# The order of loads and of square sums in the head of a four-layer trunk: x in front of the modulation tiles, its sums among the middle ones

## What is computed

```
for i in range(DEPTH):                     # mixers: conv, pool, attn, conv
    mod_p = adaln(c_ctx[None, :], ada_w[i], ada_b[i])     # silu(c) @ w + b, six blocks of 1024
    mod_s = adaln(c, ada_w[i], ada_b[i])
    hp = modulate(rms_norm(xp, norm1_w[i]), mod_p[0], mod_p[1])   # x * (1 + scale) + shift
    hs = modulate(rms_norm(xs, norm1_w[i]), mod_s[0], mod_s[1])
    ...                                    # mixer on hp and hs
    xp = xp + mod_p[2] * mp
    xs = xs + mod_s[2] * ms
    ...                                    # the same with mod 3 to 5 around a SwiGLU FFN
```

## Time and profile before

| | us |
|---|---|
| median of 3 runs | 2781.82 |
| lowest and highest | 2777.01 and 2784.19 |
| the profiled execution | 2776.66 |
| its span on the core | 2774.3 |
| mean granted TensorE clock, of 1 | 0.988 |

### The profile page before, as it was taken

One profiled execution on the slowest core, in us unless ns is written; L12 is line 12 of the kernel. 1 busy time (PEld: TensorE's weight loads), 2 busy tenths in 40 slices (PEclk: granted clock), 3 DMA queues, 4 the chain that ended last, 5 costly groups with the idle time before them and its releaser, 6 DMA issues.

```text
span 2774.3 us, 46075 instructions
## 1 busy us (share of the span) xinstructions
PE 2675.9 (96%) x17562; PEld 2605.7 (94%) x17562; DVE 1756.7 (63%) x3033; ACT 859.0 (31%) x1174; POOL 103.2 (4%) x199
## 2 busy tenths in 40 slices
PE   7998999999969999999988999999999999999997
PEld 7998999999959999999954999999999999999996
DVE  6888868775587776746665477767465554334344
ACT  3222332322343223124345332231242233223122
POOL 1000000000000000000000000000000000000000
PEclk9999999999989999999999999999999999999998
DMA  7344335343113443412100334434122222222111
GB/s 282 129 140 147 128 126 179 129 159 108 46 52 129 141 158 133 152 66 80 50 1 0 114 129 144 159 128 152 66 78 76 76 69 76 76 76 76 69 68 61
DMA packets 84442, 293.31 MB, mean 106 GB/s; under 512 B 9984, under 2 KB 12416, under 8 KB 84224
## 3 DMA queue, kind: packets, MB, share of 16 engines
q1 hardware_dynamic: 58000, 196.09, 20.7%
q0 software_dynamic: 26352, 95.96, 10.0%
HBM read 289.13 MB, written 2.88 MB: 105 GB/s over the span
## 4 chain that ended last, share of the span: by engine, by line
PE 89%; DVE 6%; ACT 2%; issue 2%; DMA 1%; DVEq 0%; ACTq 0%; POOL 0%; POOLq 0%
PE ps L395 50%; PE ps L394 34%; PE ps_x L502 1%; PE ps L481 1%; DVE w_lo L843 1%; DVE tmp L914 1%; ACT w_hi L595 1%; DVE g_lo L857 1%; DVE tmp L922 1%; DMA ada_w<-in_ada_w 1%; PE ps_sum L492 0%; DVE ps_x L871 0%; ACT tmp L736 0%; PE ps_x L469 0%; ACT g_hi L607 0%
## 5 line engine op out<-in xcount | busy, mean ns | idle before, releaser
L843 DVE TENSOR_TENSOR w_lo<-raw,w_hi 128x1024 fp32r<-128x1024 f32 (+2 forms) x364 | 430.9, 1184 | 687.0 <-ACT w_hi L595 682.9
L595 ACT ACTIVATE w_hi<-raw 128x1024 fp32r<-128x1024 f32 (+2 forms) x364 | 373.5, 1026 | 937.8 <-PE ps L395 937.4
L395 PE MATMUL ps<-h_hi,w_hi 128*128 128x386 f32 x1904 | 649.6, 341 | 0.0
L395 PE MATMUL ps<-h_lo,w_hi 128*128 128x386 f32 x1904 | 645.8, 339 | 0.0
L395 PE MATMUL ps<-h_hi,w_lo 128*128 128x386 f32 x1904 | 644.1, 338 | 0.0
L394 PE MATMUL ps<-h_hi,w_hi 128*128 128x256 f32 x1904 | 546.7, 287 | 22.1 <-DVE h_lo L978 14.9
L394 PE MATMUL ps<-h_lo,w_hi 128*128 128x256 f32 x1904 | 536.4, 282 | 0.0
L394 PE MATMUL ps<-h_hi,w_lo 128*128 128x256 f32 x1904 | 536.2, 282 | 0.0
L871 DVE CUSTOM_DVE_ANT_0 ps_x<-ada_w,cond 128x1024 f32<-128x1024 f32 x366 | 450.6, 1231 | 47.1 <-DVE tmp L914 16.4
L394 PEld LDWEIGHTS ps<-h_hi,w_hi 128*128 128x128 f32 x1904 | 361.4, 190 | 28.9 <-DVE h_lo L978 12.9
L395 PEld LDWEIGHTS ps<-h_hi,w_hi 128*128 128x128 f32 x1904 | 361.2, 190 | 3.0 <-issue 2.0
(11 more groups left out here) (123 smaller groups left out, 2736.4 us busy)
## 6 DMA issues: line engine op xcount, KB each, us to landing
raw<-in_weights SPq DMA_DIRECT2D x324, 512.0 KB, 3.2
ada_w<-in_ada_w POOLq DMA_DIRECT2D x183, 512.0 KB, 3.5
raw<-in_weights SPq DMA_DIRECT2D x32, 384.0 KB, 2.9
mix<-in_ada_head SPq DMA_DIRECT2D x9, 512.0 KB, 8.9
x<-in_x SPq DMA_DIRECT2D x4, 640.0 KB, 9.8
out_y<-mix SPq DMA_DIRECT2D x8, 320.0 KB, 2.3
cond<-in_cond SPq DMA_DIRECT2D x1, 1024.0 KB, 4.8
raw<-in_weights SPq DMA_DIRECT2D x8, 128.0 KB, 2.3
```

The costliest lines, as they stand in the source:

```text
L395: mm = pe.matmul(ps[:, 2 * slot + 1, 0:width - TA], w[:, slot, ws], a(k)[:, TA:width], start=begin, stop=end)
L595: act.activation(w_hi[:, j % 2, 0:tiles * P], raw[:, j, 0:tiles * P], ACT.Copy).then_inc(w_hi_ready, 1)
L843: dve.tensor_tensor(w_lo[:, j % 2, 0:tiles * P], raw[:, j, 0:tiles * P], w_hi[:, j % 2, 0:tiles * P].bitcast(F32), ALU.subtract).then_inc( ...
```

## The change

On SP, tables and all of x are issued right after head tile 0, and tiles 1 to 8 follow; units 2 and 3 (with rope, cache_v and all behind them) wait for PE's last tile. On GpSimd, triples 1 and 2 are written out as before, and triple 3 and later ones wait for PE's last tile. On PE, two sums each stand in front of tiles 3 to 6 instead of 5 to 8. Nothing is added to or taken from the computation.

```
+SUM_FROM = 3
...
-            for n in range(ADA_PE):
+            load_head(0)
+            load_consts()
+            for n in range(X_PIECES):
+                piece = slice(n * KD // X_PIECES, (n + 1) * KD // X_PIECES)
+                sp.dma_start(x[:, piece, :], d["x"][:, piece, :]).then_inc(x_in, 16)
+            for n in range(1, ADA_PE):
                 if n > 1:
 
                     sp.wait_ge(ada_step, 2 * n - 2)
                 load_head(n)
-                if n == 1:
-                    load_consts()
-                if 0 < n <= X_PIECES:
-                    piece = slice((n - 1) * KD // X_PIECES, n * KD // X_PIECES)
-                    sp.dma_start(x[:, piece, :], d["x"][:, piece, :]).then_inc(x_in, 16)
                 if n == ADA_PE - 3:
                     load_raw(0, (0, 1))
+
+            sp.wait_ge(head_tile, ADA_PE)
             load_raw(0, (2, 3))
...
-            with pool.Fori(1, attn_q) as i:
+            for i in range(1, ADA_HEAD):
+                for j in range(ADA_N):
+                    load_ada(i, j)
+
+            pool.wait_ge(head_tile, ADA_PE)
+            with pool.Fori(ADA_HEAD, attn_q) as i:
                 for j in range(ADA_N):
                     load_ada(i, j)
...
-                if n == ADA_PE - KD // 2:
+                if n == SUM_FROM:
                     pe.wait_ge(ones_ready, 2)
-                if n >= ADA_PE - KD // 2:
-
-                    for m in (2 * (n - ADA_PE) + KD, 2 * (n - ADA_PE) + KD + 1):
+                if SUM_FROM <= n < SUM_FROM + KD // 2:
+
+                    for m in (2 * (n - SUM_FROM), 2 * (n - SUM_FROM) + 1):
                         sum_squares(0, m)
```

## The result

| | before | changed |
|---|---|---|
| median, us | 2779.01 (12 runs) | 2783.15 (12 runs) |
| lowest and highest | 2776.41, 2784.19 | 2780.00, 2789.80 |
| ratio, 95% interval | | 1.0016, 1.0008 to 1.0023 |
| profiled execution | 2776.66 | 2783.87 |
| its span | 2774.3 | 2781.8 |

The changed kernel is 0.16% slower, 4.1 us by the medians. That is within the 0.3% that I called no change, and of the sign and about the size of the forecast (+3.2).

The account below looks back on a forecast made before the run. The prediction took PE, not loads, to bound the head's last 17.6 us. Its terms, 0 + 3 + 0 + 0.2 = +3.2 us on the first product's start, took the median from 2781.82 to 2785.0, range 2778 to 2793.

Parts of the forecast that it names:

- PE bounds the head from 31.5 us: Head before the first product: PE, not its loads, binds from 31.56 to 49.15 us, without a break.
- Rival B: Head: loads, not PE, set the end, so the change gains 8 us, to 2774; chance 5%.
- Tile 1 behind x: Head loads: x complete at 21.5 us, tile 1 lands at 23.8; PE idle 11.6 us instead of 5.2.
- The warm tiles 3 and 4 against the idle time: PE's head: 6.4 us more idle against 3.8 saved by two tiles at full clock; +2.8 us by the count of ends.
- The cold tail: Last three head tiles, no sums after: clock falls near 51.5 us, +0 to 0.4; upper end +3.8.
- rival D: Last three head tiles: clock falls right away, two tiles cost 1.89 us more each; +7 in all, 2789; chance 8%.
- The first unit: Behind the first product: no cost of its own forecast; everything there simply moves along with the first product.
- When the clock rises: First square sums in the head: clock may rise up to 3.4 us later, 0 to +1.7; 0 to +1 taken.
- Rival C: Head: clock does not rise in the first sums, every part behind them at half clock; +23 us, 2805; chance 4%.
- The loads put off: Loads issued after PE's last head tile: unit 2 and triple 3 hidden by 3.5 to 8 us, cost 0.
- The sum: Start of the first product: 0 + 3 + 0 + 0.2 = +3.2 us, all behind it moving along; median 2785.0.

Follow-up runs that it names:

- e3: Kernel before with only PE's order changed, two sums ahead of tiles 3 to 6; 2782.20 against 2777.58 us, ratio 1.0005.
- e4: Changed kernel with head tile 1 issued ahead of tables and x again; 2779.62 us against 2777.58 for the kernel before, ratio 1.0002.
- e5: Changed kernel with 11 filler matmuls in PE's wait behind tile 0; 2781.34 us against 2778.66 for the kernel before, ratio 1.0007.
- e2: Kernel before with only the queue order changed, tables and x ahead of tiles 1 to 8; 2783.75 against 2777.58 us, ratio 1.0018.
- e1: Kernel before with only the late loads put off until PE's last head tile; 2778.46 against 2777.58 us, ratio 1.0000.
- e10: As e11, plus 11 filler matmuls behind tile 0 and 3 behind tile 8; 2787.90 us, ratio 1.0035 against the kernel before.
- e11: Changed kernel with two sums ahead of tiles 1 and 2, one ahead of 3 to 6, sums not awaiting tile loads; ratio 1.0036 against the kernel before.
- e6: Kernel before with late loads put off, last two sums behind the last tile, and fillers as in e8; 2776.50 against 2778.66 us, ratio 0.9991.
- e7: Kernel before with late loads put off and last two sums behind the last tile, no fillers; 2776.51 against 2778.66 us, ratio 0.9992.
- e8: Kernel before with 17 filler matmuls in PE's waits for loads in the head; 2779.03 against 2778.66 us, ratio 0.9999.
- e9: As e8, with late loads put off, 4 fillers instead of 1 behind tile 4, 3 behind tile 8; 2776.13 against 2777.25 us, ratio 0.9989.

## Why the prediction was right, and where it was off

**PE bounds the head from 31.5 us.** Right. In the changed kernel the loads of all nine tiles are there at 39.8 us by the trace, 2.7 us sooner than before, and the last tile still ends at 53.1. Rival B falls.

**Tile 1 behind x.** Right in kind, 0.8 us off: PE starts on it at 24.59 (23.8 was forecast). x itself was 0.6 late. My count of KB took the pace of the old stream, and the old stream had more of the queue to itself at that place; that is an argument, not a measurement.

**The warm tiles 3 and 4 against the idle time.** Right: 6.99 us for tiles 1 and 2, then sums from 31.43 and tiles of 1.68. The two sides of the sum stood at 6.4 and 3.8. The measured idle time was 12.35, 7.2 more than before's 5.2. The other side measured 3.9: PE was busy for 17.7 us ahead of the sums before and for 10.4 after, 7.3 less, and has two warm tiles more behind them, 3.4. With the cold tail that gives 7.2 - 3.9 + 0.76 = 4.0, the +3.95 at the first product. (The forecast's 3.57 is from the timeline and its 1.68 from the chain; by the timeline alone they are 3.57 and 1.84, and between other tiles 3.45 and 1.70. The error is small and did not matter here.)

**The cold tail.** The place was right (a fall near 51.5; it was 51.83), the size too small: 0.76 instead of 0.2. In e3, e4 and e5 it was 2.5, 2.7 and 2.9 in the chain, with the same three tiles at the end, so that how much of rival D comes true differs from one profiled execution to the next.

**The first unit.** This step was missing. The prediction took all behind the first product as moved along. But the clock had fallen as before and rose only after 6.1 us of products instead of 3.4, and 1.22 us more were lost there in this execution. How often that happens is not known; in e2 it rose after 3.5 us.

**When the clock rises.** The term "up to 3.4 us later, 0 to +1.7" was mis-sized. e1, e3 and e4 show 12.8, 12.8 and 12.6 us from the first sum to the rise instead of 3.4, and in e1 that is 4.6 us at the first product. The two profiles compared here (3.4 and 3.3) did not have it. It can strike both kernels: e1 has PE's order of before and e4 the changed one. So it belongs to the scatter first of all; whether it also moved the difference of the medians was not measured. Rival C, the clock that stays down, had this mechanism, and its price was too high since it took the clock to stay down to the end.

**The loads put off.** Right: nothing waited, and e1 is even with before.

**The sum.** +3.95 at the first product against +3.2; 4.1 by the medians, 7.2 between the two profiled executions. The forecast of 2785.0 stood on the median of the three runs shown (2781.82), and 12 runs put that at 2779.01; so the time came out 1.9 lower while the step was 0.9 higher. That the forecast time is so near is in part luck: a base 2.8 us too high and a step 0.9 us too small worked against each other. And that +3.95 at the first product agrees with 4.1 by the medians is no proof that all of the loss lies there, since the two profiled executions are 7.2 us apart, the one of before 2.4 us under its median and the changed one 0.7 over its own. What stands by itself is the sign and the cause: e2, with the queue order alone, is slower by 1.0018 (1.0008 to 1.0028).

## What to carry to other kernels

Before moving a load forward, ask what is pushed back by it and which engine has the work that it releases: here the engine that bounds the head sat idle for 12 us behind a transfer that nobody needed yet. Count matmul time at the clock that the matmuls around it bring: narrow matmuls ran at half pace by themselves and at full pace beside wide ones, so that spreading the wide ones (two ahead of each tile) was worth more than starting them early. And where a kernel's runs scatter by a few us, read the durations of equal instructions in the profile before explaining a difference of that size.

## What the runs showed of the hardware

- Matmuls of two columns with a weight load each did not raise TensorE's clock from 1.2 to 2.4 GHz in 13.8 us without a gap (e2). In the kernel before I had seen 7 us of it. Once it was up, it fell in a row of three such tiles 4.5 us after the last wide matmul in the changed kernel and 2.6, 2.5 and 2.2 us after it in e3, e4 and e5.
- With one sum of 640 columns between two tiles it fell too (e10 at 33.1, e11 at 40.1), and in e10 it stayed at half through three more such sums and tiles. With two sums between two tiles, and no wait, it did not fall in any profile here.
- From the first sum to the rise it took 3.3 to 5.3 us in seven profiled executions (before, changed, e2, e5, e6, e7, e11) and 12.6 to 12.8 in three (e1, e3, e4). In those three the stretch in between held two pairs of sums with a tile between. e1 has the order of before on PE.
- In e8 a wait of 2.9 us on PE was followed by a fall within 0.7 us; in e9 a wait of 0.5 us at the same place was not.
- The granted clock of the records reads 1.00 for all of the time ahead of the first rise, although a tile takes 3.57 us there and 1.68 later. Up to that point only durations tell the clock.
